# The MoE token sums as two half-width tables, with each block scattered as two transfers

## The chip, the cores and the metric

One core of a Trainium2 chip runs the whole program in one launch. The metric is the time of the program on the device in microseconds (us). All numbers below are of that one core.

## What is computed

The kernel computes one layer of a hybrid encoder on 1024 tokens of width 1024 in fp32: a layer norm, a mixer of four branches, a second layer norm, and then a mixture of experts (MoE) with a residual and a last layer norm. Only the MoE part matters here. Cut to its core, the reference is:

```python
idx, w = route(xf, w_router, router_bias)          # 6 of 64 experts for each token
# for each expert e, its tokens in blocks of 128 rows:
xb = xf[tok]                                       # gather of token rows
hid = silu(xb @ wg[e]) * (xb @ wu[e])              # 1024 -> 256, twice
yb = (hid @ wd[e]) * w[..., None]                  # 256 -> 1024, scaled by the token's weight
acc = acc.at[tok].add(yb)                          # added into the tokens' rows
...
h = layer_norm(DEEPNORM_ALPHA * h + routed + shared, ln2_g, ln2_b)
```

There are 6 x 1024 = 6144 pairs of a token and an expert, some 96 for each of the 64 experts.

## The kernel before

The first 1290 us or so are the norms, the mixer and its merge; the change doesn't touch them. The expert stage follows. It runs one block of up to 128 token rows for each of the 64 experts, then one more block (AHEAD is 1) and a short loop over any further blocks, for experts with more than 128 tokens. Block b is written as b = 4 i + c; the functions below take (i, c). The stage's code stands once for each engine, in `experts`:

- SyncE (SP) loads each expert's three weight matrices, 1 MB each, into one of four slots, as soon as the slot is free (`load_gate_up`, `load_down`).
- GpSimd (POOL) first issues four indirect transfers that gather the token rows of block b+3 in pieces of 256 columns, 1 KB for each row (`gather_rows`, the transfer at L3171), and then one indirect transfer that adds block b-1's results into the tokens' rows (`scatter_rows`, L3179).
- VectorE (DVE) makes the lists of rows and turns the gathered rows (L3185), TensorE (PE) multiplies by gate and up (L3192, 16 matmuls), transposes the hidden rows (L3200) and multiplies by down (L3208, 8 matmuls), and makes the next list's sums (L2803).
- The result of block b-1, 128 x 1024, leaves the two PSUM banks in halves of 512 columns: ScalarE (ACT) scales the first half (L3014, counted by the semaphore `ya`), DVE the second (L2915, counted by `yb`). They write one of two buffers, `w.y[c % 2]`.

The sums of all tokens lie in `g.sums`, one table of 1024 x 1024 fp32 values in HBM. `begin_sum` (L2248, on SP's queue) stores there what each token has already, residual and shared expert, in 8 transfers of 512 KB. `scatter_rows` then adds 128 rows of 4 KB to it; rows of a block that hold no token have an index beyond the bounds and are skipped. Since two blocks can hold the same token, a scatter may be issued only when the one before it has landed: `scatter` waits for `ya`, `yb`, the row list (`to`) and the landing of the previous block's scatter (`stored`). A result may be written only when the scatter that last read its buffer, two blocks earlier, has landed: `result` on ACT and on DVE waits for that.

After the 64 blocks, POOL's `after` and the loop behind it run the remaining blocks in turn: scatter, four gathers, a wait for the scatter's landing; `rest_scatter` at the end issues the last scatter. When that has landed (`ended`), `finish` loads the sums in 8 transfers of 512 KB (L3237), normalizes them on DVE and ACT, and stores the output.

What orders the work around the change: POOL's queue holds, block after block, four gathers and a scatter, and every wait on it holds what stands behind. All indirect transfers go through one queue of the DMA engines, which the profile calls q0; the weights go through another, q1. Both run on the same 16 DMA engines.

## Time and profile before

| | us |
|---|---|
| median of three runs | 2063.26 (2061.43 to 2064.11) |
| the profiled execution's own time | 2062.23 |
| its span, first to last instruction | 2060.5 |
| PE busy | 1992.8 (97%) |
| DVE busy | 1139.9 (55%) |
| POOL busy | 778.1 (38%) |
| ACT busy | 504.8 (24%) |
| DMA, mean over the span | 180 GB/s |
| DMA, in the expert stage from 1300 to 1845 us | 357 GB/s |

PE is busy nearly all the time, up to the last 60 us. A busy share alone doesn't say what sets the end, because the matmuls' ends are modelled; the chain of waits does. It is read from the last instruction backwards: at each step to what released it. For an indirect transfer, the row of POOL is the time in which its descriptors (the list of moves for the DMA engines) are written; the data move after that, and show in the view of the DMA queues and in the waits for the landing.

### The profile page before, as it was taken

The numbers are of one execution on the slowest core, as the hardware profiler recorded it, in microseconds if no ns is written. First come the engines' busy times: TensorE is split into PE (matmuls) and PEld (weight loads), VectorE is DVE, ScalarE is ACT, GpSimd is POOL, SyncE is SP. The second block draws the span as 40 slices with busy tenths as digits, with TensorE's granted clock in tenths as the row PEclk, the third lists the DMA queues.
The fourth block names the chain that finished last, engine by engine and source line by source line (L and its number), as shares of the span: only waits on it lengthen the run. The fifth ranks groups of instructions, "written<-read, shape, count | busy, mean of one in ns | idle before, by whom it ended". The sixth has DMA issues, their size and how long they took to land.

```text
span 2060.5 us, 23760 instructions
## 1 busy us (share of the span) xinstructions
PE 1992.8 (97%) x7237; PEld 1013.2 (49%) x7238; DVE 1139.9 (55%) x3065; ACT 504.8 (24%) x1102; POOL 778.1 (38%) x717
## 2 busy tenths in 40 slices
PE   8999999999999999999999999999999999999992
PEld 6444667575544444444445554444444444444440
DVE  6222546776621222335676656966666666666645
ACT  3111554452322222314432230111111111111113
POOL 1762005622122221115980002554545545455541
PEclk9999999999999999999999999999999999999996
DMA  5421000011132222144353006999999999999964
GB/s 148 133 86 41 21 21 22 22 47 47 46 129 76 72 82 77 54 123 171 103 207 140 37 31 258 362 361 349 357 359 352 358 358 352 355 349 351 358 206 172
DMA packets 129639, 370.45 MB, mean 180 GB/s; under 512 B 33712, under 2 KB 65668, under 8 KB 103832
## 3 DMA queue, kind: packets, MB, share of 16 engines
q1 hardware_dynamic: 103960, 314.83, 40.8%
q0 software_dynamic: 23520, 54.61, 10.9%
q8 instruction: 44, 0.72, 0.1%
q10 hardware_dynamic: 2080, 0.01, 0.1%
q14 instruction: 35, 0.29, 0.0%
HBM read 320.57 MB, written 68.17 MB: 189 GB/s over the span
## 4 chain that ended last, share of the span: by engine, by line
PE 40%; DMA 7%; POOL 3%; issue 3%; DVE 2%; ACT 0%; SPq 0%; POOLq 0%; DVEq 0%
PE banks L3192 17%; PE banks L3208 8%; DMA sums<-arena,row_to 6%; PE banks L2289 4%; PE banks L2336 3%; POOL arena L2136 2%; PE banks L2014 2%; PE banks L2352 1%; PE banks L279 1%; PE banks L2803 1%; PE banks L2312 1%; PE banks L3200 1%; DMA arena<-in_w_router_dram 0%; DVE arena L3268 0%; DVE arena L3185 0%
## 5 line engine op out<-in xcount | busy, mean ns | idle before, releaser
L3192 PE MATMUL banks<-arena 128*128 128x512 f32 x1056 | 468.8, 597 | 3.3 <-DVE arena L3185 0.8
L3171 POOL DMA_INDIRECT arena<-h_rows,index x268 | 280.0, 1045 | 140.4 <-issue 77.8
L3192 PEld LDWEIGHTS banks<-arena 128*128 128x128 f32 x1056 | 195.2, 190 | 226.3 <-issue 224.8
L1720 PE MATMUL banks<-arena 128*128 128x512 f32 x672 | 299.0, 594 | 1.1 <-ACT arena L323 1.1
L3208 PE MATMUL banks<-arena 128*128 128x512 f32 x528 | 237.6, 593 | 1.3 <-ACT arena L3007 0.8
L3179 POOL DMA_INDIRECT sums<-arena,row_to x66 | 108.0, 1636 | 272.2 <-DMA sums<-arena,row_to 231.9
L3185 DVE STREAM_TRANSPOSE arena<-arena 128x1024 f32<-128x1024 f32 x66 | 133.9, 2029 | 119.8 <-PE banks L3192 115.1
L279 PE MATMUL banks<-arena 128*128 128x512 f32 x416 | 191.8, 598 | 2.5 <-PEq L108 2.2
L1720 PEld LDWEIGHTS banks<-arena 128*128 128x128 f32 x672 | 123.1, 190 | 135.6 <-issue 134.0
L3155 DVE TENSOR_SCALAR index<-row 32x1 uint32<-32x1 f32 x1072 | 155.4, 145 | 17.1
L3208 PEld LDWEIGHTS banks<-arena 128*128 128x128 f32 x528 | 100.2, 190 | 127.0 <-issue 125.3
L777 PE MATMUL banks<-arena 128*128 128x512 f32 x336 | 145.0, 593 | 0.2 <-DVE arena L689 0.2
L285 PE MATMUL banks<-arena 128*128 128x256 f32 (+1 forms) x640 | 143.8, 366 | 0.0
L3002 ACT ACTIVATE arena<-banks 128x256 f32<-128x256 f32 x65 | 25.0, 384 | 414.8 <-PE banks L3192 400.9
L2014 PE MATMUL banks<-arena 128*128 128x512 f32 x280 | 120.6, 592 | 0.1
L285 PEld LDWEIGHTS banks<-arena 128*128 128x128 f32 x640 | 105.4, 190 | 19.2 <-issue 10.1
L2289 PE MATMUL banks<-arena 128*128 128x512 f32 x256 | 112.7, 594 | 1.5 <-POOL arena L2136 1.5
L279 PEld LDWEIGHTS banks<-arena 128*128 128x128 f32 x416 | 74.3, 190 | 74.6 <-issue 72.8
L777 PEld LDWEIGHTS banks<-arena 128*128 128x128 f32 x336 | 63.5, 190 | 80.3 <-issue 78.4
L3014 ACT ACTIVATE arena<-banks,weight 128x512 f32<-128x512 f32 x64 | 44.0, 688 | 217.4 <-PE banks L3208 139.9
L2915 DVE TENSOR_SCALAR arena<-banks,weight 128x512 f32<-128x512 f32 x64 | 48.0, 751 | 88.6 <-PE banks L3208 51.2
L2014 PEld LDWEIGHTS banks<-arena 128*128 128x128 f32 x280 | 53.1, 190 | 67.5 <-issue 64.8
(400 smaller groups left out, 2431.9 us busy)
## 6 DMA issues: line engine op xcount, KB each, us to landing
arena<-in_w_exp_gate_dram SPq DMA_DIRECT2D x66, 1024.0 KB
arena<-in_w_exp_up_dram SPq DMA_DIRECT2D x66, 1024.0 KB
arena<-in_w_exp_down_dram SPq DMA_DIRECT2D x66, 1024.0 KB
arena<-in_w_in_dram SPq DMA_DIRECT2D x26, 1024.0 KB, 5.3
gates<-arena SPq DMA_DIRECT2D x60, 256.0 KB, 2.0
arena<-gates SPq DMA_DIRECT2D x15, 1024.0 KB, 7.7
arena<-h_rows,index POOLq DMA_INDIRECT x268
arena<-in_x_dram SPq DMA_DIRECT2D x8, 512.0 KB, 5.8
```

Source lines behind the costliest of these rows:

```text
L279: mm = pe.matmul(bank[0:width], w[:, q, col:col + width], g.hT[:, q, at * HALF:(at + 1) * HALF], start=(q == 0), stop=(q == KT - 1))
L285: mm = pe.matmul(bank[:, m * width:(m + 1) * width], g.hT[:, k, (at + m) * P:(at + m + 1) * P], w[:, k, col:col + width], start=(k == 0), ...
L777: mm = pe.matmul(block_bank(n, b), left[:, k, :], right[:, k, :], start=(alone and k == 0), stop=(k == 3), skip_group_check=True)
L1720: mm = pe.matmul(gate_bank(n, b), left[:, k, :], right[:, k, :], start=(alone and k == 0), stop=(k == 3), skip_group_check=True)
L2014: mm = pe.matmul(product_bank(n, c), lhs[:, k, :], rhs[:, k, :], start=(alone and k == 0), stop=(k == deep[b] - 1), skip_group_check=True)
L2289: mm = pe.matmul(bank[:, mix_bank(m) + h, :], merged[:, k, m * P:(m + 1) * P], wout[k][:, h * HALF:(h + 1) * HALF], start=(k == first), st ...
L3155: ins = dve.tensor_scalar(g.index[32 * b:32 * b + 32, k, q:q + 1], g.row[32 * q:32 * q + 32, k, :], 4.0, float(b), ALU.mult, ALU.add)
L3171: return pool.indirect_dma_start(w.x[k][:, 256 * q:256 * (q + 1)], None, rows, bass.IndirectOffsetOnAxis(ap=g.index[:, k, q:q + 1], axis=0 ...
L3179: return pool.indirect_dma_start(g.sums, bass.IndirectOffsetOnAxis(ap=g.row_to[:, b:b + 1], axis=0), w.y[k], None, bounds_check=last, oob_ ...
L3185: return dve.transpose(w.xT.rearrange("p k (q n) -> p q k n", q=4), w.x[k].rearrange("p (q n k) -> p q k n", q=4, k=KT))
L3192: mm = pe.matmul(g.bank[:, 2, :].rearrange("p (a f) -> p a f", a=2), xT[:, k, :], wgu[:, :, k, :], start=(k == 0), stop=(k == KT - 1))
L3208: mm = pe.matmul(g.bank[:, 4 + h, :], hidT[:, k, :], wdn[:, k, h * HALF:(h + 1) * HALF], start=(k == 0), stop=(k == 1))
```

## The change

`g.sums` becomes two tables of 1024 x 512, one for each half of the columns. `scatter_half` takes the place of `scatter_rows` and adds 128 rows of 2 KB to one table. `scatter` waits for the row list and the previous block's landing first, then for `ya` and issues the first half, then for `yb` and issues the second. Both halves count into the same semaphore, so its values double: 32 for a block where it was 16. The stores that begin the sums and the loads of `finish` are split likewise, 16 transfers of 256 KB each where there were 8 of 512 KB.

```diff
-    g.sums = nc.dram_tensor("sums", [T, D], F32, kind="Internal").ap()
+    g.sums = [nc.dram_tensor(f"sums{h}", [T, HALF], F32, kind="Internal").ap() for h in range(2)]
...
             sp.wait_ge(s["base"], m + 1)
-            sp.dma_start(g.sums[m * P:(m + 1) * P, :], base[:, m, :]).then_inc(g.sums_begun, 16)
+            for h in range(2):
+                sp.dma_start(g.sums[h][m * P:(m + 1) * P, :],
+                             base[:, m, h * HALF:(h + 1) * HALF]).then_inc(g.sums_begun, 16)
...
             def result(i, c):
                 act.wait_ge(s["down"], val(i, c) + 1)
                 if has(i, c, -2):
-                    act.wait_ge(stored[c % 2], half(i, c) * 16)
+                    act.wait_ge(stored[c % 2], half(i, c) * 32)
...
             def scatter(i, c):
-                pool.wait_ge(s["ya"], val(i, c) + 1)
-                pool.wait_ge(s["yb"], val(i, c) + 1)
                 pool.wait_ge(s["to"], 2 * val(i, c) + 2)
                 if has(i, c, -1):
-                    pool.wait_ge(stored[(c + 1) % 2], 16 * (half(i, c) + c % 2))
+                    pool.wait_ge(stored[(c + 1) % 2], 32 * (half(i, c) + c % 2))
                 else:
-                    pool.wait_ge(g.sums_begun, 16 * NT)
-                scatter_rows(g, pool, w, c % 2, c % 4).then_inc(stored[c % 2], 16)
+                    pool.wait_ge(g.sums_begun, 32 * NT)
+                for h, ready in enumerate((s["ya"], s["yb"])):
+                    pool.wait_ge(ready, val(i, c) + 1)
+                    scatter_half(g, pool, w, c % 2, c % 4, h).then_inc(stored[c % 2], 16)
 
             def rest_scatter(n, done):
-                pool.wait_ge(v["ya"], n)
-                pool.wait_ge(v["yb"], n)
-                scatter_rows(g, pool, w, 0, 0).then_inc(done, 16)
+                for h, ready in enumerate((v["ya"], v["yb"])):
+                    pool.wait_ge(ready, n)
+                    scatter_half(g, pool, w, 0, 0, h).then_inc(done, 16)
...
-def scatter_rows(g, pool, w, k, b):
+def scatter_half(g, pool, w, k, b, h):
     first, last = w.bounds
     pool.reg_add(last, first, T - 1)
-    return pool.indirect_dma_start(g.sums, bass.IndirectOffsetOnAxis(ap=g.row_to[:, b:b + 1], axis=0), w.y[k], None,
+    return pool.indirect_dma_start(g.sums[h],
+                                   bass.IndirectOffsetOnAxis(ap=g.row_to[:, b:b + 1], axis=0),
+                                   w.y[k][:, h * HALF:(h + 1) * HALF], None,
                                    bounds_check=last, oob_is_err=False, compute_op=ALU.add)
...
-        sp.wait_ge(ended, 16)
+        sp.wait_ge(ended, 32)
         for m in range(NT):
-            sp.dma_start(z[:, m, :], g.sums[m * P:(m + 1) * P, :]).then_inc(sum_in[m], 16)
+            for h in range(2):
+                sp.dma_start(z[:, m, h * HALF:(h + 1) * HALF], g.sums[h][m * P:(m + 1) * P, :]).then_inc(sum_in[m], 16)
```

The other waits on these semaphores double in the same way.

## Rows read from the trace of the kernel before

**Rows 1.** Table by stage: window, its length, busy us of each engine, clock, DMA share, GB/s.
```profile
1300.00:1845.00 545.00, 540.96 (x1664) 255.64 (x1664) 369.08 (x1235) 66.22 (x147) 280.75 (x244) 1.00 1.01 357
```

**Rows 2.** Chain that ended last, shares by line: first of 1400 to 1600 us, then 1845 to 1958 us.
```profile
by line: PE banks L3192 63.9%; PE banks L3208 31.1%; PE banks L2803 2.8%; PE banks L3200 2.0%; issue 0.4%
...
by line: DMA sums<-arena,row_to 93.6%; issue 5.5%; DVE arena L3185 1.8%; POOLq L3178 0.3%; POOLq L3169 0.2%; POOLq L3049 0.2%; POOLq L3051 0.2%; POOLq L2730 0.2%; POOLq L3061 0.1%
```

**Rows 3.** Timeline of PE (start us, length us, engine, line, operation), two stretches.
```profile
1625.46 7.10 PE L3192 MATMUL banks<-arena 128*128 128x512 f32 x16
...
1648.00 1.53 PE L3192 MATMUL banks<-arena 128*128 128x512 f32 x3
...
1669.78 5.39 PE L3192 MATMUL banks<-arena 128*128 128x512 f32 x12
...
1935.59 7.10 PE L3192 MATMUL banks<-arena 128*128 128x512 f32 x16
...
1960.03 2.38 PE L3192 MATMUL banks<-arena 128*128 128x512 f32 x5
```

**Rows 4.** Timelines of ACT and POOL: result and scatter of two blocks, the scatter of a third.
```profile
1414.65 0.69 ACT L3014 ACTIVATE arena<-banks,weight 128x512 f32<-128x512 f32 x1 [3.21 <-PE banks L3208]
...
1421.54 1.61 POOL L3179 DMA_INDIRECT sums<-arena,row_to  x1 [4.15 <-DMA sums<-arena,row_to]
...
1845.33 1.61 POOL L3179 DMA_INDIRECT sums<-arena,row_to  x1 [5.21 <-DVE arena L3185]
...
1937.55 0.69 ACT L3014 ACTIVATE arena<-banks,weight 128x512 f32<-128x512 f32 x1 [5.38 <-DMA sums<-arena,row_to]
...
1949.47 1.62 POOL L3179 DMA_INDIRECT sums<-arena,row_to  x1 [4.35 <-DMA sums<-arena,row_to]
```

**Rows 5.** POOL's costliest groups by line: count, busy us, mean ns, idle before and its releasers.
```profile
L3171 POOL DMA_INDIRECT arena<-h_rows,index x268 | 280.0, 1045 | 140.4 <-issue 77.8 <-DVE index L3155 60.8 <-DVE arena L2915 0.9
L3179 POOL DMA_INDIRECT sums<-arena,row_to x66 | 108.0, 1636 | 272.2 <-DMA sums<-arena,row_to 231.9 <-DVE arena L2915 13.0 <-issue 11.7
```

**Rows 6.** DMA queues in four windows: 1258-1268 (four gathers), 1996.5-2001 (one scatter), 1905.7-1908.2, 1908.3-1913.
```profile
q0 software_dynamic: 192, 0.46, 15.9%
...
q0 software_dynamic: 144, 0.45, 68.7%
...
q0 software_dynamic: 11, 0.00, 0.3%
...
q1 hardware_dynamic: 133, 0.96, 52.6%
q0 software_dynamic: 127, 0.47, 51.1%
```

**Rows 7.** Timeline of POOL: the scatter of 1903 us and the last part of the stage.
```profile
1903.53 1.63 POOL L3179 DMA_INDIRECT sums<-arena,row_to  x1 [5.02 <-DMA sums<-arena,row_to]
...
1994.72 1.62 POOL L3179 DMA_INDIRECT sums<-arena,row_to  x1 [4.54 <-DVE arena L2915]
2001.70 1.57 POOL L3179 DMA_INDIRECT sums<-arena,row_to  x1 [5.36 <-DMA sums<-arena,row_to]
...
2015.78 1.56 POOL L3179 DMA_INDIRECT sums<-arena,row_to  x1 [5.59 <-issue]
...
2022.99 1.61 POOL L3179 DMA_INDIRECT sums<-arena,row_to  x1 [0.30 <-issue]
```

**Rows 8.** The last result (timeline of DVE), the last landing (chain), the loads of `finish` (timelines).
```profile
2021.03 0.75 DVE L2921 TENSOR_SCALAR arena<-banks,weight 128x512 f32<-128x512 f32 x1 [1.92 <-PE banks L3208]
...
2022.99 4.61 DMA sums<-arena,row_to
...
2027.61 4.42 SPq L3237 DMA_DIRECT2D arena<-sums  x8
...
2032.07 1.06 ACT L3298 ACTIVATE arena<-arena 128x1024 f32<-128x1024 f32 x1 [10.36 <-DMA arena<-sums]
```

**Rows 9.** Timeline of POOL: the first scatter, behind the gathers of its step.
```profile
1304.63 1.65 POOL L3179 DMA_INDIRECT sums<-arena,row_to  x1 [0.30 <-issue]
```

More of the change, by code:

```diff
@@ L2912, in result @@
                 if has(i, c, -2):
-                    dve.wait_ge(stored[c % 2], half(i, c) * 16)
+                    dve.wait_ge(stored[c % 2], half(i, c) * 32)
                 dve.wait_ge(s["to"], 2 * val(i, c) + 2)
@@ L3080, in after @@
             def after():
-                pool.wait_ge(stored[0], 16 * (NE // 2))
+                pool.wait_ge(stored[0], 32 * (NE // 2))
                 pool.sem_inc(v["free"], 1)
                 pool.wait_ge(s["to"], 2 * NB)
-                pool.wait_ge(stored[1], 16 * (NE // 2))
+                pool.wait_ge(stored[1], 32 * (NE // 2))
             count = []
@@ L3094, in _ @@
                     gather_rows(g, pool, w, 1, q).then_inc(v["gathered"], 16)
-                pool.wait_ge(v["stored"], (o + 1) * 16)
+                pool.wait_ge(v["stored"], (o + 1) * 32)
                 pool.sem_inc(v["free"], 1)
@@ L3245, in first_tile @@
         def first_tile():
-            dve.wait_ge(sum_in[0], 16)
+            dve.wait_ge(sum_in[0], 32)
             for h in range(2):
@@ L3296, in scalar @@
         for m in range(1, NT):
-            act.wait_ge(sum_in[m], 16)
+            act.wait_ge(sum_in[m], 32)
             act.activation(scratch[0], z[:, m, :], ACT.Copy, accum_out=total[:, m:m + 1]).then_inc(s["to"], 1)
```

## The prediction, made before the change was timed

> **What bounds the kernel now.** I read the table by stage first, then the chain of waits by stretch, then the timelines of POOL and PE, and last the DMA queues. From 1300 to 1845 us PE is busy 540.96 of 545 us, and the 16 DMA engines are full as well, at 357 GB/s [rows 1]. The chain decides which of the two counts: between 1400 and 1600 us it runs through PE's matmuls alone, between 1845 and 1958 us it is 93.6% landings of the scatter [rows 2]. So the stage changes its owner late. Up to 1845 us PE sets the pace. From there the chain "wait for the previous landing, issue, write descriptors, move, land" sets it.
>
> The rhythms say by how much. PE starts four blocks in 1669.78 - 1625.46 = 44.32 us, 11.08 each; the two of them that hold the loop's turn take 1648.00 - 1625.46 = 22.54 us [rows 3]. The 13 scatters from 1845.33 to 1994.72 take 11.49 us each [rows 4, 7]. The scatter falls behind its result: by 1421.54 - 1414.65 = 6.9 us early, by 1949.47 - 1937.55 = 11.9 us late [rows 4]. With two buffers a lag of 12 us means that the result two blocks on must wait for the landing, and there ACT is indeed released by the DMA, after 5.38 us idle [rows 4]. PE feels it once: two blocks from 1935.59 to 1960.03 take 24.44 us instead of 22.54, so 1.9 us are lost [rows 3].
>
> After the last block of the loop five scatters follow one another: at 1994.72, 2001.70, one more, 2015.78 and 2022.99 us [rows 7]; the last one lands after 4.61 us, and `finish` loads its tables at once [rows 8]. What the change can touch is therefore the late chain, this tail, and the loads behind it.
>
> **The change, part by part.**
>
> *Writing descriptors.* Today one scatter takes POOL 1.61 us, and a gather of the same 128 rows, 1 KB each, 1.00 to 1.04 us [rows 5, 7]. No row shows an accumulate of 2 KB rows. Its bounds are 1.0 (the gather) and 1.6 us (the scatter of 4 KB rows). I take 1.05 for each half, since the DMA view speaks for cost by pieces: a gather leaves 48 packets in the queue, 192 for four [rows 6], which is 32 of data, one for every four rows of 1 KB, and 16 that report completion, one for each DMA engine; a scatter leaves 144, that is 128 of 4 KB and 16 of completion, in 0.45 MB with the skipped rows nearly empty. Between two indirect transfers POOL idles 0.30 us [rows 7, 9]. The pair costs 1.05 + 0.30 + 1.05 = 2.40 us, 0.79 more than today, and the first half's descriptors are ready 0.56 us earlier.
>
> *Moving rows, DMA engines full.* From 1908.3 to 1913 us both queues are served one packet each in turn, 133 of the weights against 127 of q0. A scatter packet costs 0.511 x 16 x 4.7 / 115 = 0.33 us of an engine (0.47 MB are 115 rows), a weight packet 0.526 x 16 x 4.7 / 133 = 0.30 us [rows 6]. An engine has 8 rows of a full block, so their move takes at least 8 x 0.63 = 5.0 us. A packet evidently holds 4 KB, four gather rows or one scatter row. If it then holds two rows of 2 KB, both halves together have today's 128 data packets. New are 16 completion packets, one more turn on each engine: 0.01 + 0.30 = +0.31 us. Is there a bubble between the halves? The second half's descriptors are ready 1.35 us after the first's, and the first half keeps an engine busy for 4 x 0.63 = 2.5 us, so no. In the late stretch the queue is empty when the scatter comes: its descriptors were written by 1905.16, and from 1905.7 to 1908.2 us q0 has 11 packets and no bytes worth a digit [rows 6, 7]. There the earlier first half moves the whole train forward. The chain changes by -0.56 + 0.31 = -0.25 us for each scatter, over 13 scatters -3.2 us. The bounds are 0 and -0.56 x 13 = -7.3 us with the faster descriptors; with slow ones see below.
>
> The Trainium skill ("DMA: Bandwidth & Descriptors", section "SWDGE vs HWDGE vs iDMA") says that a packet has at most 4096 B preferably and up to 64 descriptors, and that an engine changes queues only between packets. The gathers' packets agree; for accumulating rows no run here shows it, and if it held for them the sum would stay as it is.
>
> *The tail.* Here the engines are otherwise idle. One scatter to the next takes 2001.70 - 1994.72 = 6.98 us. Writing costs +0.79, but when the second half is written, half of the data have been moved: -4 x 0.33 = -1.32. That is -0.5 us for each of three intervals, -1.6 us. The interval to the last scatter differs. It holds a scatter and four gathers back to back on POOL, 7.21 us [rows 7], and grows by the full +0.79 us. The last scatter's 4.61 us have few rows to hide anything behind: +0.79 us as the upper bound, which I take (the lower is 0).
>
> *What is late next.* If the scatters come 3.2 + 1.6 = 4.8 us earlier, PE takes over. The last result is written at 2021.03 + 0.75 = 2021.78 us [rows 8] after PE's own sequence, in which only the 1.9 us above are waits for a scatter. The last scatter cannot start before 2021.78 - 1.9 + 0.3 = 2020.2 us; the scatter chain alone would allow 2022.99 - 4.8 + 0.8 = 2019.0. So its start moves from 2022.99 to 2020.2, -2.8 us, and its landing by -2.8 + 0.8 = -2.0 us. More than about 2.8 us can't be had here however fast the chain becomes.
>
> *Order on POOL.* The gathers stand behind both halves and start 0.8 us later. Their rows are needed two blocks on, more than 20 us, so this is free; without that distance it would be 0.8 us a block. The new order of waits holds nothing either: behind the wait for `yb` stand the second half, the next gathers and, through their rows, PE; but the scatter comes 7 to 12 us after ACT's half [rows 4], DVE's half takes 0.75 us [rows 8], and both are long done. Issuing each half as soon as it is scaled is worth nothing in the stage.
>
> *Stores and loads.* Eight more stores go to SP's queue, ahead of weights and spread over the token tiles. For each I take the 4.42 / 8 = 0.55 us that an issue takes SP in `finish` [rows 8]; the four slots of weights cover it, and without them the last store would delay one block by 0.55 us. The first scatter doesn't wait for them, it starts 0.30 us after a gather [rows 9]. Sixteen loads instead of eight take SP 8.8 us, but DVE and ACT work through the tiles one after another. Only tile 0 and 1 count, between 2027.61 and 2032.07 [rows 8]: bounds 0 and +1.1 us (two more issues); I take +0.3, for the bytes are the same.
>
> **The sum.** -2.0 + 0.3 = -1.7 us. On the profiled execution's own 2062.23 us that is 2060.5. This execution lies 1.0 us under the median of the runs, 2063.26, so I forecast 2061.5 us. Its own range, from the bounds: 2059.5 (no cost of landing and loads) to 2064.5 us (no gain in the chain: -1.6 + 0.8 + 0.8 + 0.3, and the loads at their worst).
>
> **The rivals.**
>
> *Slow descriptors.* Each half costs POOL 1.6 us, because writing is paid by row, not by byte; 128 rows remain 128 rows. For it: nothing separates the two in the trace except the accumulate, and the gather's rows are cheaper at the same count. Against it: a scatter row moves four times the bytes. The first half is then no earlier and the extra turn stays: 13 x 0.31 = +4.0 us. In the tail +1.9 - 1.3 = +0.6 for three intervals, +1.8; to the last scatter +1.9, its landing +1.9, loads +0.3. Together +9.9 us, 2073 us. Were the chain in charge from the first scatters on, it would be up to 61 x 0.31 = 19 us instead of 4, 2088.
>
> *One row, one packet (the slower side).* An accumulating row may need its own packet, whatever its length; today's counts can't tell, because 4 KB fill a packet anyway. Then each engine has 8 more turns for a full block, each against a weight packet: +8 x 0.30 = 2.4, less 0.25, 2.2 us for each scatter. It decides as soon as the chain exceeds PE's 11.08 us, which it does now by 0.4 (11.49 against 11.08). Over 13 scatters that is +28 us, 2092; over all it would be 130 us, but a stretched stage leaves the weights' queue empty part of the time, and then a turn costs nothing. I take 2092, with 2075 to 2130 as its range.
>
> *The halves don't overlap.* The second starts moving when the first has landed. Its price is at least what lies between the last scatter's descriptors and its landing, 4.61 - 1.61 = 3.0 us [rows 7, 8], for 13 scatters and 5 of the tail: +54 us, about 2117. Against it: gathers of one block queue up behind each other, 192 packets without such gaps [rows 6]. The Trainium skill (the same page, section "Anatomy of one DMA — SWDGE (gpsimd) path") gives a transfer from POOL about 2.0 us fixed besides its bytes; paid in full for 66 more transfers that would be 132 us, by an estimate from that page. The tail's 3.0 us agree with such a fixed part; whether a second transfer pays it again no row shows.
>
> *The chain lets go altogether.* The lag stays at 7 us, PE never waits, and the last landing costs nothing extra: -2.8 us from above and +0.3 for the loads, 2063.3 - 2.5 = 2060.8 us; with nothing for the loads 2060.5. Faster by over 4 us would need PE's own blocks to shorten, and nothing in the change does that; DVE's and POOL's shared work might, as an accident.
>
> **Chances.** The forecast has 0.45, the free chain 0.07, slow descriptors 0.22, one packet a row 0.18, no overlap 0.04, and something faster than PE's sequence allows 0.04. A measurement of this kernel can tell about 0.2%, 4.1 us: the borders are 2059.1 and 2067.4 us. The forecast and the free chain lie within them except for 0.02 below; slow descriptors lie within for 0.03. So faster 0.06, same 0.53, slower 0.41. The range goes from 2059 us up to where the packets' case begins to weigh, 2090 us, and leaves out some 0.06 below and 0.13 above.
>
> **What would show it.** Right: two POOL rows near 1.05 us for a scatter; 16 more packets of q0 for a scatter, 160 and not 288; the late scatters under 11.3 us apart; PE's start of two blocks near 22.5 us also around 1940; the last scatter near 2020 us. Wrong: rows of 1.6 us; a q0 with twice the data packets; landings that release ACT long before 1845 us; PE's blocks over 11.5 us in the middle of the stage. The prediction fails most surely if the middle stretch, which PE owns by a few tenths of a microsecond only, passes to the scatter.

## The result, and the profile after

The changed kernel takes 2105.78 us (median of 4 runs, 2103.10 to 2107.12), the kernel before, run beside it, 2062.78 us (2061.43 to 2064.11). The medians are 43 us apart. The ratio estimated from all the runs is 1.020, with a 95% interval of 1.0187 to 1.0213, that is 39 to 44 us slower. Forecast were 2061.5 us, with 2090 as the upper end. What two of the rivals assumed, "slow descriptors" (2073) and "one row, one packet" (2092), is found in the trace, both at once; neither rival was priced in the right place.

The profiled execution has a span of 2101.2 us against 2060.5. Its table by stage, for the same window as [rows 1] (us, busy us of PE with its matmuls, PEld, DVE, ACT, POOL, clock, DMA share, GB/s):

```profile
1300.00:1845.00 545.00, 536.45 (x1586) 252.73 (x1585) 347.10 (x1171) 63.11 (x140) 368.12 (x275) 1.00 1.00 341
```

PE looks as busy as before, 536 us against 541, but it has done 1586 matmuls and not 1664, 4.7% fewer; the DMA engines are as full as before, and move 341 GB/s and not 357. A busy share doesn't show this loss, the counts and the bytes do. Where it comes from stands in the groups by line and in the waits between 1300 and 2030 us:

```profile
L3173 POOL DMA_INDIRECT arena<-h_rows,index x268 | 318.9, 1190 | 136.2 <-issue 79.3 <-DVE index L3157 55.9 <-ACT arena L3016 0.6
L3181 POOL DMA_INDIRECT sums<-arena,row_to x132 | 212.6, 1610 | 173.3 <-issue 88.6 <-DMA sums<-arena,row_to 71.1 <-DVE arena L2917 10.3
...
ACT arena L3016 <- DMA sums<-arena,row_to: 366.6, 56, 8.8
DVE arena L2917 <- DMA sums<-arena,row_to: 211.9, 53, 5.5
```

L3181 is the scatter. A half costs POOL 1.61 us, as much as the whole did [rows 5]. L3016 and L2917 scale a block's result. ACT waits 56 times for a landing, 366.6 us in all; in the same view of the kernel before there were nine such waits, of 42.1 us, and it was PE that ACT waited for. The scatter chain (wait for the previous landing, issue, write, move, land) owns the stage almost from its beginning.

The timeline of POOL says when. These are first halves (for 1610.82 and 2052.71 also what follows):

```profile
1305.05 1.64 POOL L3181 DMA_INDIRECT sums<-arena,row_to  x1 [0.30 <-issue]
...
1433.39 1.63 POOL L3181 DMA_INDIRECT sums<-arena,row_to  x1 [1.69 <-issue]
...
1610.82 1.63 POOL L3181 DMA_INDIRECT sums<-arena,row_to  x1 [3.48 <-DMA sums<-arena,row_to]
1612.75 1.58 POOL L3181 DMA_INDIRECT sums<-arena,row_to  x1 [0.30 <-issue]
1614.64 1.87 POOL L3173 DMA_INDIRECT arena<-h_rows,index  x1 [0.30 <-issue]
...
1877.89 1.63 POOL L3181 DMA_INDIRECT sums<-arena,row_to  x1 [1.54 <-issue]
...
2028.87 1.62 POOL L3181 DMA_INDIRECT sums<-arena,row_to  x1 [3.50 <-DVE arena L2917]
...
2036.59 1.57 POOL L3181 DMA_INDIRECT sums<-arena,row_to  x1 [4.22 <-issue]
...
2052.71 1.56 POOL L3181 DMA_INDIRECT sums<-arena,row_to  x1 [4.40 <-DMA sums<-arena,row_to]
2054.57 1.56 POOL L3181 DMA_INDIRECT sums<-arena,row_to  x1 [0.30 <-issue]
...
2061.76 1.63 POOL L3181 DMA_INDIRECT sums<-arena,row_to  x1 [0.30 <-issue]
```

Beside the same scatters of the kernel before, this accounts for the whole difference of 40.7 us between the two spans:

| stretch | before | after | more |
|---|---|---|---|
| start to the first scatter | 1304.63 [rows 9] | 1305.05 | 0.4 |
| first to 11th scatter | to 1421.54 [rows 4]: 116.9 | to 1433.39: 128.3 | 11.4 |
| 11th to 49th, 38 intervals | to 1845.33 [rows 4]: 11.15 each | to 1877.89: 11.70 each | 20.7 |
| 49th to 62nd, 13 intervals | to 1994.72 [rows 7]: 11.49 each | to 2028.87: 11.61 each | 1.6 |
| 62nd to 66th, the tail | to 2022.99 [rows 7]: 28.3 | to 2061.76: 32.9 | 4.6 |
| last scatter to the loads of `finish` | to 2027.61 [rows 8]: 4.6 | to 2067.36: 5.6 | 1.0 |
| the rest | | | 1.0 |

Only 8.2 us lie where the prediction looked (the 13 late scatters, tail, last landing, loads). 32.1 us lie in the stretch that it gave to PE.

The last question is what went through the queues. Here is the DMA view of two windows, 2036.6 to 2044.8 us (one block's two transfers, nothing else) and 1615.5 to 1621.4 us (mostly a block's rows, under full load); the columns are packets, MB and share of 16 engines:

```profile
q0 software_dynamic: 288, 0.31, 32.1%
...
q0 software_dynamic: 319, 0.63, 51.5%
q1 hardware_dynamic: 134, 1.03, 49.7%
```

288 packets are 256 rows and twice 16 of completion: in the trace's records each accumulated row of 2 KB is a packet of its own, while four gathered rows of 1 KB are one [rows 6]. The Trainium skill ("DMA: Bandwidth & Descriptors", section "SWDGE vs HWDGE vs iDMA") lets a packet hold up to 4096 B and up to 64 descriptors. The records of accumulating rows don't show this; packets filled to 4096 B would have been 160. The 319 packets of the second window are, by their sizes, 233 rows of 2 KB, 38 gather packets of 4 KB and 48 of completion; of the 134, 126 carry weights.

### The profile page after: what moved, and what is told of

Read it like the earlier page. It is cut to its first block and busy times, and to the rows that moved or that the text cites. A ratio compares the mean times of both kernels' runs of the same rounds, so it can differ in the third digit from the quotient of the medians.

```text
span 2101.2 us, 23870 instructions
## 1 busy us (share of the span) xinstructions
PE 2020.0 (96%) x7237; PEld 1025.7 (49%) x7238; DVE 1134.1 (54%) x3065; ACT 504.9 (24%) x1102; POOL 921.4 (44%) x783
## 5 line engine op out<-in xcount | busy, mean ns | idle before, releaser
L3173 POOL DMA_INDIRECT arena<-h_rows,index x268 | 318.9, 1190 | 136.2 <-issue 79.3
L3196 PEld LDWEIGHTS banks<-arena 128*128 128x128 f32 x1056 | 195.2, 190 | 226.5 <-issue 224.7
L3181 POOL DMA_INDIRECT sums<-arena,row_to x132 | 212.6, 1610 | 173.3 <-issue 88.6
L1720 PEld LDWEIGHTS banks<-arena 128*128 128x128 f32 x672 | 123.1, 190 | 135.9 <-issue 134.0
L2917 DVE TENSOR_SCALAR arena<-banks,weight 128x512 f32<-128x512 f32 x64 | 48.0, 750 | 229.7 <-DMA sums<-arena,row_to 214.7
L3212 PEld LDWEIGHTS banks<-arena 128*128 128x128 f32 x528 | 100.2, 190 | 127.2 <-issue 125.3
L3016 ACT ACTIVATE arena<-banks,weight 128x512 f32<-128x512 f32 x64 | 44.0, 687 | 391.7 <-DMA sums<-arena,row_to 369.9
L285 PEld LDWEIGHTS banks<-arena 128*128 128x128 f32 x640 | 105.4, 190 | 19.2 <-issue 10.1
L279 PEld LDWEIGHTS banks<-arena 128*128 128x128 f32 x416 | 74.3, 190 | 74.6 <-issue 73.0
L777 PEld LDWEIGHTS banks<-arena 128*128 128x128 f32 x336 | 63.5, 190 | 80.3 <-issue 78.4
L1680 POOL TENSOR_TENSOR arena<-arena 128x512 f32<-128x512 f32 x12 | 15.2, 1269 | 165.2 <-DMA arena<-in_w_in_dram 145.7
```

The costliest lines, as they stand in the source:

```text
L279: mm = pe.matmul(bank[0:width], w[:, q, col:col + width], g.hT[:, q, at * HALF:(at + 1) * HALF], start=(q == 0), stop=(q == KT - 1))
L285: mm = pe.matmul(bank[:, m * width:(m + 1) * width], g.hT[:, k, (at + m) * P:(at + m + 1) * P], w[:, k, col:col + width], start=(k == 0), ...
L777: mm = pe.matmul(block_bank(n, b), left[:, k, :], right[:, k, :], start=(alone and k == 0), stop=(k == 3), skip_group_check=True)
L1720: mm = pe.matmul(gate_bank(n, b), left[:, k, :], right[:, k, :], start=(alone and k == 0), stop=(k == 3), skip_group_check=True)
L3173: return pool.indirect_dma_start(w.x[k][:, 256 * q:256 * (q + 1)], None, rows, bass.IndirectOffsetOnAxis(ap=g.index[:, k, q:q + 1], axis=0 ...
L3181: return pool.indirect_dma_start(g.sums[h], bass.IndirectOffsetOnAxis(ap=g.row_to[:, b:b + 1], axis=0), w.y[k][:, h * HALF:(h + 1) * HALF] ...
```

## The experiments

"More" is against the median of the kernel before, timed in the same session (2065.35, 2063.40, 2063.11 and 2063.82 us). The ratio and its interval are estimated from all the runs and not from the two medians; they differ from the quotient of the medians by up to 3 us, and the interval is 2 to 5 us to either side.

**Writing, landing, packets: one more empty transfer.** Each of the first four puts a transfer into the kernel before whose 128 rows are all skipped (every index is out of bounds). It costs POOL's writing and 144 packets, and moves nothing. Their core, at three places:

```diff
+                pool.reg_add(w.bounds[1], w.bounds[0], T - 1)
+                pool.indirect_dma_start(g.void, bass.IndirectOffsetOnAxis(ap=g.nowhere[:, 0:1], axis=0), g.ident[:],
+                                        None, bounds_check=w.bounds[1], oob_is_err=False,
+                                        compute_op=ALU.add).then_inc(spare, 16)
                 scatter_rows(g, pool, w, c % 2, c % 4).then_inc(stored[c % 2], 16)
```

Two of them ahead of the scatters of the first three blocks only:

> The kernel before, with two empty transfers (all 128 indices out of bounds, to a table nobody reads) on POOL ahead of the scatters of blocks 0, 1 and 2 only; nothing of the computation changes. Three theories of the 43 us that the change costs. Pace: the chain of scatters keeps PE's 11.08 us only while it is less than about 10 us behind the results, and once it is 12 us behind it runs at 11.5 to 11.7 us and never catches up; then a delay of some 3 x 3.8 us at the start alone costs most of the loss: 2085 to 2105 us, with ACT released by landings from the first tens of blocks on. Packets: each scatter pays for 128 more data packets; here there are none, 2063 us. Writing: each scatter pays for 1.9 us of descriptors inside the chain; three scatters cost at most 11 us, 2063 to 2074 us.

Measured: 2075.03 us, 9.7 more, ratio 1.006 [1.0041, 1.0078]. A delay at the start alone doesn't cost most of the loss.

One ahead of each scatter:

> The kernel before, with one empty transfer ahead of every scatter, after the wait for the previous landing: all rows of the scatter are written 1.9 us later (or less, if an empty 512 B row is cheaper to write), with the old packets of 4 KB. Writing: the chain takes 1.9 us more for each scatter, 11.5 + 1.9 = 13.4 us, so 60 x 2.3 = +140 us less what a relieved weights' queue gives back; at least the change's +43 us. Pace: as that, since lag and latency both grow: 2120 to 2200 us. Packets: the same data packets as before, so within 10 us of before.

Measured: 2101.79 us, 36.4 more, 1.0181 [1.0163, 1.0199]. The data packets are the same as before, and yet this costs nearly the change's loss, though less than writing or pace were expected to.

One behind each scatter, its landing awaited by nobody:

> The kernel before, with one empty transfer behind every scatter and before the gathers, whose landing nobody waits for: POOL has the second transfer's writing, the queue its 16 completion packets and 128 empty ones, but the chain of scatters doesn't contain it. Writing: no loss, 2063 us. Packets: no loss but for the turns of small packets, 2063 to 2070 us. Pace: only what POOL is late with in the first blocks, where its gathers stand close to their indices: 2063 to 2095 us.

Measured: 2080.95 us, 15.6 more, 1.0082 [1.0061, 1.0104], above what writing or packets were expected to cost.

One behind each scatter, aimed at the table of sums with rows of 4 KB, its landing counted like the scatter's:

> The kernel before, with an empty transfer of 4 KB rows (all out of bounds) behind every scatter, and its landing counted like the second half's in the change: writing, completion and order on POOL are the change's, the data packets are before's 128 of 4 KB. Writing: the whole loss, 2100 to 2110 us. Pace: most of it, 2085 to 2110 us. Packets: the data packets of 2 KB make the loss, so here 2063 to 2070 us.

Measured: 2095.50 us, 30.2 more, 1.0156 [1.0132, 1.0181]. The groups by line, of the kernel with the uncounted and of the one with the counted transfer:

```profile
L3070 POOL DMA_INDIRECT void<-ident,nowhere x64 | 100.7, 1574 | 19.5 <-issue 19.2 <-DVE weight L2902 0.3
...
L3069 POOL DMA_INDIRECT sums<-arena,nowhere x64 | 101.5, 1586 | 19.5 <-issue 19.5
```

Rows of 512 B and rows of 4 KB, none of which moves its data, take POOL 1.57 and 1.59 us: writing an accumulate is paid by row. And a second transfer without any data costs 30.2 of the change's 43 us if its landing is waited for, and half of that if not. The other 12.8 us are in part the tail, which has no empty transfers: its five scatters take 28.5 us there (2025.25 to 2053.79) and 32.9 in the changed kernel. What the data of the second transfer add in the stage wasn't measured by itself.

The disturbed start explains little. After it ACT waits for landings as often as in the changed kernel (waits, 1300 to 2030 us), and yet this costs 9.7 us:

```profile
ACT arena L3018 <- DMA sums<-arena,row_to: 329.7, 58, 6.5
```

So a lag by itself costs some 10 us, and once. Its 38 steps from the 11th to the 49th scatter take 11.24 us each (1433.34 to 1860.31), against 11.70 in the changed kernel; what counts is how much longer than PE's the chain's step is.

**The wait for both landings.** The changed kernel, with each table's landings counted on a semaphore of its own, so that a half waits only for its own table, and ACT and DVE only for the half that each of them writes:

```diff
-                if has(i, c, -1):
-                    pool.wait_ge(stored[(c + 1) % 2], 32 * (half(i, c) + c % 2))
-                else:
-                    pool.wait_ge(g.sums_begun, 32 * NT)
-                for h, ready in enumerate((s["ya"], s["yb"])):
+                for h, (ready, landed) in enumerate(((s["ya"], stored), (s["yb"], stored2))):
+                    if has(i, c, -1):
+                        pool.wait_ge(landed[(c + 1) % 2], 16 * (half(i, c) + c % 2))
+                    elif h == 0:
+                        pool.wait_ge(g.sums_begun, 32 * NT)
                     pool.wait_ge(ready, val(i, c) + 1)
-                    scatter_half(g, pool, w, c % 2, c % 4, h).then_inc(stored[c % 2], 16)
+                    scatter_half(g, pool, w, c % 2, c % 4, h).then_inc(landed[c % 2], 16)
```

> The change, but each table has its own chain: the first half of a block waits only for the previous first half's landing, the second half only for the previous second half's. Same transfers, packets and writing; only the wait for both landings is taken apart. Pace theory (the chain's latency decides, most of it the wait for the first packets and one landing after the other): the first half is released some 2 us earlier, the chain gets under PE's 11.08 us again, 2060 to 2075 us. Packets theory (the queue's throughput, 256 data packets a block, decides): no relief, 2100 to 2108 us. Writing theory: the second half's 1.9 us leave the chain, 2062 to 2075 us.

Measured: 2073.25 us, 9.8 more than before, 1.0054 [1.0037, 1.0070], and so gives back some 33 of the change's 43 us. Same tables, same packets, same writing; packets alone, which expected no relief, can't be the whole cause. What is left of ACT's and DVE's waits (waits, 1300 to 2030 us):

```profile
ACT arena L3017 <- DMA sums<-arena,row_to: 32.5, 9, 4.2
DVE arena L2918 <- DMA sums<-arena,row_to: 128.1, 41, 5.1
```

ACT waits 9 times and not 56. Three quarters of the loss hang on the two halves being tied to one another's landing; whether in POOL's wait or in those of ACT and DVE isn't told, since the run unties both. DVE, which writes the second half, still waits for a landing 41 times (53 in the changed kernel): the second half's chain isn't free.

**Is it the full queue?** Of the expert weights only a quarter of the bytes is loaded from the fifth block on, in the kernel before and in the changed one:

```diff
-    sp.dma_start(g.region(at, 2048), expert_plane(g, e, "w_exp_gate")).then_inc(done, 16)
+    n = 2048 if isinstance(e, int) and e < 4 else 512
+    sp.dma_start(g.region(at, n), expert_plane(g, e, "w_exp_gate")[:, 0:n]).then_inc(done, 16)
```

(and the same for the other two planes)

> The kernel before, with a quarter of the weight bytes loaded from the fifth expert on (512 of 2048 columns of each plane; the rest of the slot keeps older values, so the result is another): the weights' queue is then mostly empty. All theories: the chain of scatters falls to 7 to 9 us, PE owns the stage throughout, and nothing is behind at the end: 3 us under before, 2058 to 2062 us.

> The change, with the same quarter of the weight bytes. If the loss needs the full weights' queue (pace and packets theories), only the tail's cost of writing is left, 2 to 6 us over the light kernel before: 2062 to 2067 us. If the writing alone made it (1.9 us more in a chain that the weights don't slow), PE still covers it: the same number, so this pair tests whether the weights' queue is part of the cause at all; a loss of 20 us or more here would say that it is not.

Measured: 2063.07 us (0.9996 [0.9986, 1.0005]) and 2063.94 us (1.0000 [0.9991, 1.0010]). Three readings follow. The kernel before doesn't become faster when its scatters are hardly ever late: they come 1.8 us behind ACT's result there (1417.37 to 1419.16) and not 6.9. It was at PE's pace, and by the interval's lower end a better scatter could have gained 3 us at most. Second, the change costs nothing that can be measured under light weights: the 16 engines are 63% busy there from 1400 to 1845 us and not 100%. The light packets of weights also carry 2 KB each and not 8, so this pair doesn't tell a full queue from long packets in it. Third, timelines of PE around the block where before lost time, of before and then of the light one:

```profile
1948.17 7.11 PE L3192 MATMUL banks<-arena 128*128 128x512 f32 x16
...
1938.33 7.10 PE L3194 MATMUL banks<-arena 128*128 128x512 f32 x16
1945.27 3.60 PE L3210 MATMUL banks<-arena 128*128 128x512 f32 x8
1948.71 0.39 PE L3202 MATMUL banks<-ident,arena 128*128 128x128 f32 x2
1950.87 7.11 PE L3194 MATMUL banks<-arena 128*128 128x512 f32 x16
...
1961.74 7.10 PE L3194 MATMUL banks<-arena 128*128 128x512 f32 x16
```

The first of the two steps takes 12.54 us also where nothing waits for a landing (1938.33 to 1950.87; before: 1935.59 [rows 3] to 1948.17, 12.58). Only the second, 11.86 us against 10.87, was lost to the scatter.

The delay under full weights can be seen directly. Here is the DMA view of the changed kernel from 1612.5 to 1614.5 us, right after the first half's writing ended at 1612.45, then of the light one from 1608.2 to 1609.2 us, after the same moment at 1608.15:

```profile
q1 hardware_dynamic: 120, 0.86, 103.6%
q0 software_dynamic: 5, 0.00, 0.7%
...
q0 software_dynamic: 44, 0.05, 63.3%
q1 hardware_dynamic: 71, 0.11, 35.5%
```

With full weights the 2 us behind the writing move nothing of the scatter, by when the second half is written as well; with light ones its rows are on their way within 1 us (44 packets, 0.05 MB). So issuing the first half early gains nothing where the queue is full.

The same quarter of the bytes for the blocks 4 to 8 alone (gate and up of 5 to 8, down of 4 to 7), in the changed kernel:

> The change, with a quarter of the weight bytes for blocks 4 to 8 alone (the rest of those slots keeps older values, so the result is another); from then on the weights are whole. The scatters get through the start without falling behind. If the chain has two paces and the start chooses (a lag of 12 us is never made good, a small one stays small): 2066 to 2080 us. If each scatter of the stage costs its share whatever the start: the lag is back at 12 us within some 15 blocks, at 11.7 us a block the end comes at 2095 to 2104 us.

Measured: 2097.92 us, 34.8 more, 1.0159 [1.0142, 1.0176]. Its sixth scatter is early, at 1362.98 us; the 21st has fallen back to within 3 us of the changed kernel's (timeline of POOL, first the light start, then the change):

```profile
1362.98 1.62 POOL L3187 DMA_INDIRECT sums<-arena,row_to  x1 [3.19 <-DMA sums<-arena,row_to]
...
1548.48 1.62 POOL L3187 DMA_INDIRECT sums<-arena,row_to  x1 [2.60 <-issue]
...
1374.25 1.62 POOL L3181 DMA_INDIRECT sums<-arena,row_to  x1 [4.23 <-DMA sums<-arena,row_to]
...
1551.32 1.62 POOL L3181 DMA_INDIRECT sums<-arena,row_to  x1 [2.08 <-issue]
```

Of 11.3 us ahead 2.8 are left after 15 blocks. The loss isn't chosen by the start, it is paid block by block.

**Half the data.** In the loop only the first 512 columns are scattered, 128 packets of 2 KB a block in place of 256; the other half is left out:

```diff
-                for h, ready in enumerate((s["ya"], s["yb"])):
-                    pool.wait_ge(ready, val(i, c) + 1)
-                    scatter_half(g, pool, w, c % 2, c % 4, h).then_inc(stored[c % 2], 16)
+                pool.wait_ge(s["ya"], val(i, c) + 1)
+                pool.wait_ge(s["yb"], val(i, c) + 1)
+                scatter_half(g, pool, w, c % 2, c % 4, 0).then_inc(stored[c % 2], 32)
```

> The change without its second half: each block of the 64 scatters only its first 512 columns (the second half of the routed sums of these blocks is left out), one transfer of 128 packets of 2 KB; writing and packet count are before's, the bytes are half. The deferred blocks still scatter both halves. Packets theory: as before or better, 2058 to 2066 us. Pace theory: the data phase is shorter by some 1.3 to 2.6 us, the chain stays under PE's 11.08 us: 2057 to 2062 us. Writing theory: as before, 2062 us. If it were slower than before, the two tables themselves (stores, loads, rows of 2 KB in HBM) would cost something.

Measured: 2064.26 us, 1.0005 [0.9996, 1.0015]. Two tables and their 16 stores and loads cost nothing that can be measured; the second transfer of a block is the cost. Since the bytes are halved too, the run doesn't say what 256 rows of 2 KB cost against 128 of 4 KB.

**Time in the chain, late gathers, packets.** First come delays by register additions on POOL, 45 between the wait for the landing and the scatter, and 90 between the scatter and the gathers:

> The kernel before, with 45 register additions on POOL between the wait for the previous landing and the scatter (an estimated 1.8 us, from some 0.04 us a register instruction in the chain of waits): pure delay inside the chain, no descriptors, no packets. If the chain's latency is the cause, this costs as much as the empty transfer ahead of the scatter: 2095 to 2110 us. If packets and descriptors in the queue are the cause: 2063 to 2072 us.

> The kernel before, with 90 register additions on POOL between the scatter and the next gathers (an estimated 3.6 us, of which 1.6 run while the scatter's descriptors are written): the gathers come some 2 us later, as behind the change's second half, with nothing in the chain and nothing in the queue. If late gathers are what the uncounted empty transfer paid for: 2075 to 2085 us. If its packets and descriptors were: 2063 to 2068 us.

Measured: 2064.01 and 2062.19 us (1.0003 and 0.9996). These tell nothing, since the delay never came: with 45 additions POOL idles for 4 us before its scatter as it did without them, and with 90 the gather still starts 0.30 us after the scatter (timelines):

```profile
1612.21 1.61 POOL L3181 DMA_INDIRECT sums<-arena,row_to  x1 [4.04 <-DMA sums<-arena,row_to]
...
1609.26 1.61 POOL L3181 DMA_INDIRECT sums<-arena,row_to  x1 [4.09 <-DMA sums<-arena,row_to]
1611.17 1.04 POOL L3173 DMA_INDIRECT arena<-h_rows,index  x1 [0.31 <-issue]
```

So real work took their place, two additions of a private tile, ahead of the scatter or (as `fill_after`) behind it:

```diff
+                pool.tensor_tensor(g.spent[0][:], g.ident[:], g.ident[:], ALU.add).then_inc(spare, 1)
+                pool.tensor_tensor(g.spent[1][:], g.ident[:], g.ident[:], ALU.add).then_inc(spare, 1)
+                pool.wait_ge(spare, 2 * val(i, c) + 2)
                 scatter_rows(g, pool, w, c % 2, c % 4).then_inc(stored[c % 2], 16)
```

> The kernel before, with two additions of 128x128 on POOL (the trace shows such an operation at 0.6 to 0.7 us) between the wait for the previous landing and the scatter, and a wait for both: some 1.4 us more in the chain from landing to landing, not one packet more in any queue. If what counts is time in the chain: the late stretch of before takes 11.49 us a scatter with 1.0 us of slack short of PE's 11.08 in the early blocks, so the lag grows from the first blocks on and the stage ends like the variant with a counted empty transfer, 2080 to 2095 us. If what counts is packets in the queue: 2062 to 2067 us.

> The same two additions, behind the scatter and ahead of the next gathers: the chain of landings is untouched, the gathers are written 1.4 us later. If the 17 us that an uncounted empty transfer costs come from gathers that are written later and then move together with the scatter's rows, this gives 2073 to 2083 us; if they come from packets or from reservations in the queue, 2062 to 2067 us.

And the uncounted empty transfer behind the four gathers, where it delays nothing:

> The kernel before with the uncounted empty transfer of 512-byte rows behind the four gathers instead of ahead of them: the same packets in the same queue, nothing delayed on POOL that had not 4 us of idle time behind it. If packets cost: 2073 to 2083 us, as where it stood ahead of the gathers. If late gathers cost: 2062 to 2067 us.

Measured: 2086.29 us (22.5 more, 1.0107 [1.0090, 1.0124]), 2063.46 us (0.9997 [0.9988, 1.0007]) and 2076.07 us (12.3 more, 1.0058 [1.0042, 1.0075]). Timelines of POOL in the first and in the second:

```profile
1612.60 0.39 POOL L3066 TENSOR_TENSOR spent<-ident 128x128 bf16<-128x128 f32 x1 [2.09 <-DMA sums<-arena,row_to]
1612.96 0.39 POOL L3067 TENSOR_TENSOR spent<-ident 128x128 bf16<-128x128 f32 x1
1614.15 1.61 POOL L3184 DMA_INDIRECT sums<-arena,row_to  x1 [0.80 <-POOL spent L3067]
...
1613.27 1.61 POOL L3184 DMA_INDIRECT sums<-arena,row_to  x1 [2.62 <-DMA sums<-arena,row_to]
1614.37 0.94 POOL L3067 TENSOR_TENSOR spent<-ident 128x128 bf16<-128x128 f32 x1
...
1616.58 1.05 POOL L3176 DMA_INDIRECT arena<-h_rows,index  x1 [0.92 <-DVE arena L3190]
```

The additions don't delay by their whole length, since part of the way from a landing to the next scatter is there without them, and behind a scatter they start while it is still being written. How much they put into the chain is read from the chain of waits (start, length), of the kernel before, then of `fill_before`:

```profile
1915.55 10.76 DMA sums<-arena,row_to
...
1927.10 10.28 DMA sums<-arena,row_to
...
1603.11 9.36 DMA sums<-arena,row_to
...
1614.15 9.88 DMA sums<-arena,row_to
```

From a landing to the start of the next scatter pass 0.79 us in the first (1926.31 to 1927.10) and 1.68 in the second (1612.47 to 1614.15); over all scatters the medians are 0.85 and 1.69. So some 0.84 us more in the chain, with not one packet more, cost 22.5 us. (With the 45 register additions the median is 0.85 as well.) In `fill_after` the next gather starts 3.31 us after the scatter's start (1613.27 to 1616.58), 1.4 more than the 1.91 of the register run above, and this costs nothing. 144 packets a block without a delay on POOL cost 12.3 us; against the same packets ahead of the gathers (15.6), which come 1.9 us late there, the intervals overlap, so that late gathers add at most little. Neither cause is the only one: chain time and packets cost each by itself. How they add up isn't known. The counted empty transfer (30.2) and the one ahead of the scatter (36.4) have both, the latter with 1.9 us more in the chain (median 2.77 from landing to scatter).

**Twice the change.** Four tables, four transfers of 1 KB rows a block:

```diff
-                for h, ready in enumerate((s["ya"], s["yb"])):
+                for h, ready in enumerate((s["ya"], s["ya"], s["yb"], s["yb"])):
```

> Four tables of 256 columns and four transfers of 1 KB rows for each block. The dose is doubled: POOL writes 4 x 1.9 = 7.6 us of descriptors inside the chain, and with the gathers' 5.3 us it has 12.9 us of work for a block, more than the change's 11.7 us. Latency: the fourth is written at 7.6 us, its data start 3 us later, so the chain takes 13 to 14 us: 2105 + 55 x 1.3 to 2.3, 2175 to 2235 us. If packets paired with weight packets were the cost (8 more on each engine for each doubling, 2.4 us and then 4.8 us more): above 2300 us.

Measured: 2432.44 us, 369 more, 1.1784 [1.1764, 1.1803], far above the expectation from latency. It lies above 2300 us, as was expected if the packets were the cost, but this doesn't decide for them, for the clock fell as well. The table by stage, for the window of [rows 1], and the waits of ACT:

```profile
1300.00:1845.00 545.00, 452.06 (x1115) 201.68 (x1114) 244.20 (x816) 42.67 (x98) 353.16 (x253) 0.87 0.76 244
...
ACT arena L3016 <- DMA sums<-arena,row_to: 604.7, 40, 16.7
```

The granted clock of PE is 0.87 in this window, where it is 1.00 in the two shown before. PE is busy 452 of 545 us here, waits in every block, and part of its time runs at the lower of its two levels (1.2 and not 2.4 GHz). So some of the 369 us may be slower matmuls, and not transfers; how much wasn't separated.

## Why the prediction was wrong

*"I take 1.05 for each half."* Wrong; measured 1.61 us. The rule "cost by pieces" came from packet counts and was laid over POOL's writing, which the counts say nothing about. The rival had it right, "128 rows remain 128 rows", and had 0.22.

*"If it then holds two rows of 2 KB."* Not what the trace records: 288 packets and not 160. [Rows 6] already spoke against one size of 4 KB for all packets, for there 133 packets of the weights moved 0.96 MB, 7.2 KB each. But the rival's price, 0.30 us for each extra packet because one of the weights goes between any two, was wrong as well. Under load the change moved 271 packets of q0 with data against 126 of the weights, where in the window of [rows 6] it was 115 against 117. A row of 2 KB takes 0.18 us of an engine (median of the 233), about half of a 4 KB row's 0.33. The strict turn that [rows 6] seemed to show isn't kept with small packets. Whether an engine takes several of them in a turn, or the weights have none ready, stays open.

*"There the earlier first half moves the whole train forward", -0.56 us.* Wrong, also in its mechanism. [Rows 6] had the answer: for 2.5 us behind the writing q0 has 11 packets and no bytes. I read that as an empty queue that waits for rows, and it is the time that rows wait under full weights. The second half's writing fits into it, so writing the first half earlier gains nothing; what the split adds is the second half's landing, to which everything is tied.

*"Up to 1845 us PE sets the pace", so that only 13 late scatters count.* This is the step that cost most. The reading was true for the kernel before and didn't carry to the changed one. In the kernel before POOL is already released by the previous landing 54 times for its 66 scatters (waits, 1300 to 2030 us):

```profile
POOL sums L3179 <- DMA sums<-arena,row_to: 231.9, 54, 5.4
```

And the 38 intervals from 1421.54 to 1845.33 take 11.15 us each [rows 4], against 11.08 of PE's blocks [rows 3]. The chain was thus already a little slower than PE, and PE didn't feel it, because with two result buffers a scatter may come some 12 us behind its result before the next but one must wait. In the kernel before this lag grows slowly, from 6.9 us at the 11th scatter to 11.9 at 1949 us [rows 4]. In the changed kernel it is 11.5 us at the fifth scatter already and stays near 12.4, and from there each block costs the chain's step: 11.70 us, 0.6 over PE's. `fill_before` shows how little it takes: 0.84 us more for a block cost 22.5 us. The change lost 32.1 us ahead of the late stretch and 1.6 us in it, where the chain had had the stage already. The prediction named this at its end as the way in which it would fail most surely. It had priced it twice in passing, at 2088 us under slow descriptors and at 130 us under the packets, and gave it no case of its own.

*"Two blocks take 24.44 us instead of 22.54, so 1.9 us are lost."* About half right: 12.54 us of the first step are there without any wait, 1.0 us was lost. From the first scatter to the last the kernel before takes 718.4 us (1304.63 to 2022.99) and the light one 716.9 (1307.33 to 2024.24), so some 1.4 us were to be had and not 2.8.

*The tail, "-0.5 us for each of three intervals".* Wrong in sign: 2036.59 - 2028.87 = 7.72 us against 6.98 [rows 7], +0.74; all three together take 23.84 us (to 2052.71) against 21.06 (to 2015.78), +2.8, or 0.9 each, where slow descriptors had 0.6. *To the last scatter +0.79:* measured 2061.76 - 2052.71 = 9.05 us against 7.21, +1.84, which is the 1.9 us of slow descriptors. *The last landing +0.79:* measured +1.0. *Loads +0.3:* the rest is 1.0 us in all. The chain's last piece, second half's issue to landing, is

```profile
2063.69 3.65 DMA sums<-arena,row_to
2067.36 0.33 SPq L3242
```

3.65 us with 1.58 of writing in it. 2.1 us lie between written and landed, near the 2.0 us that the Trainium skill gives as fixed ("DMA: Bandwidth & Descriptors", section "Anatomy of one DMA — SWDGE (gpsimd) path"). A second transfer doesn't pay them once more: the tail's intervals grew by 0.9 us, so the rival "the halves don't overlap" (+3.0) was wrong.

*Right were:* the gathers 0.8 us later are free (1.4 us later they still are); stores and loads cost about nothing in the stage (first scatter +0.4 us); the wait for `yb` holds nothing (the second half follows 0.30 us after the first); issuing each half when it is scaled is worth nothing.

What stays open: `own_chains` still loses 9.8 us. That is about the 12.3 us of the packets alone, and DVE's 41 waits for the second half are there as well; no run has the two apart. Nor does any run show why 144 packets without data cost 12.3 us.

## What to carry to other kernels

A chain of transfers whose step is close to the bound engine's, and which only the spare buffers hide, is to be priced over every block and not over those in which it is late already; put a microsecond of real work into it first and see what that costs. Splitting an indirect accumulate by columns multiplies POOL's writing and the packets; only the time to move a row falls (0.18 us against 0.33). If the pieces are waited for together, the last one sets the time. Before such a change ask which two buffers or engines would be released by one piece alone, and give each piece its own semaphore, or leave the transfer whole.

## What the runs showed of the hardware that I had not expected

- POOL writes an accumulating transfer of 128 rows in 1.6 us, whether the rows have 512 B, 2 KB or 4 KB and even if all are skipped (means 1.57, 1.61, 1.64 and 1.59 us); a gather of as many rows takes 1.05 on average in the kernel before [rows 5].
- Under full weights more than 2 us pass after the writing in which the scatter moves nothing (1612.45 to past 1614.5); under light weights, less than 1.
- Small packets of q0 aren't answered one by one by the other queue: 271 with data against 126.
- 45 or 90 register additions on POOL delay its transfers by nothing: from landing to scatter 0.85 us with 45 and without, the gather 0.31 us behind the scatter with 90.
